# A two-layer decoder trunk on one core: four norm sums as fp32r products, one low part made by VectorE, one Pool split held back

## The chip, the core and the metric

The kernel runs on one core of a Trainium2 chip. TensorE (PE) multiplies, VectorE (DVE) and GpSimd (POOL) work elementwise, ScalarE (ACT) applies functions and copies, SyncE (SP) issues most transfers. The metric is the device time of one execution in microseconds, and of several executions their median.

## What is computed

The reference is a trunk of two layers on a sequence of 1024 positions and a model width of 1024, all in float32:

```python
h = x
for layer in range(2):
    hn = rms_norm(h, norm_mix[layer])
    h = h + (mixer_ab(hn, ...) if layer == 0 else mixer_c(hn, ...))
    h = h + conv_ffn(rms_norm(h, norm_ffn[layer]), ...)
return rms_norm(h, norm_final)
```

`rms_norm(x, g)` is `x * rsqrt(mean(x*x) + 1e-6) * g` over the 1024 features. `mixer_ab` is one input projection, eight heads of dilated attention (A), four heads of gated linear attention in chunks (B), and one output projection. `mixer_c` is a projection with GELU, a causal 128x128 mixing of positions per channel group, a gate and an output projection. `conv_ffn` is an up projection to 2 x 2816, a causal convolution of width 3, a SiLU gate and a down projection.

## The kernel before, in words

**Layout.** Activations stand transposed: features on the 128 partitions, eight tiles `k` of 128 features, 1024 positions in the free dimension. `x` holds the residual stream. A product of float32 accuracy is made of three fp32r products: each operand is split into a high part (rounded to fp32r) and a low part (the difference), and `cross` (L923) adds high x high, high x low and low x high, for two halves of 512 positions each. So every weight tile is split before use: its high part `w_hi` (four slots of 128x1024) by POOL or ScalarE, its low part `w_lo` by POOL with a subtraction (`split`, L626; `low_part`, L635; in the FFN `low`, L692). Activations are split by ScalarE (`high`, L2462) and VectorE (`act_low`, L1646).

**A norm.** The scaling by `rstd` is applied after the product, so that the products with `x * gain` can start before the statistic is there. ScalarE squares the tiles into `sq` and, for the first, `acc` (L2466); VectorE adds them up into `acc` (`accumulate`, L1638). TensorE then sums over the partitions and spreads the sum to all of them by multiplying `ones` (128x128) with `acc`, in f32, one product for each half (`sum_squares`, L953; for the third norm it is written out at L1567 to L1571). VectorE turns the PSUM sum into a variance in `sq` (`norm_var`, L1623; L2330), ScalarE makes a first guess of `rstd` with Ln and Exp (`guess`, L2455), and VectorE refines it in three steps (`norm_refine`, L1628). There are four such norms: `norms[0]` ahead of the first mixer, `norms[1]` ahead of the first FFN, `norms[2]` ahead of mixer C, `norms[3]` ahead of the second FFN. The final norm is done in its own way (`last_sum`, L1523) and is not touched.

**Order.** Each engine's program is written out by hand, and the engines meet by counting semaphores; nothing is planned at run time. What stands around the change:

- Start (`norms[0]`). ScalarE makes the high parts of the eight activation tiles and, after the first of them, the high part of the first weight tile (L2480); POOL makes its low part (L655), which TensorE wants at `weight_low(0)` (L1104). VectorE's first work is the eight `act_low` (L1656), then the additions. POOL's further splits wait until `acc` is done (L657). TensorE does the first k projection by hand (L1101 to L1117), then the q projection, `b_project("q", 0, 0, 6)` (L1118), with the sum of squares behind tile k = 6 of 0 to 7; before the v projection it waits for the variance (L1119), since the sum stands in the PSUM banks that v writes.
- Attention. POOL's splits of the output weights (`N_WO`, L675 to L680) stand behind one another; the third, slot 2, waits for six low parts of activations (`WO.lo`). In the last head pair VectorE forms `a_quad` (`statistics_by_quadrant`, L1934, the first step of the semaphore `A.st` for that pair), and TensorE moves it with eight small products (`move_statistics`, L1270).
- FFN (`norms[1]`, `norms[3]`). `first(0)` and `first(1)` (L1429) are two whole tiles of the up projection; in `first(1)` the sum of squares stands behind k = 1. Then follow 21 pairs of tiles (`pair`, L1455), which are computed with seven products of half tiles each in place of eight: P1, P2, P6, P5, P7, P3, P4 in this order. Each pair has four weight slots with a low part by POOL each: GA (needed by P1), GB (by P6), GC (by P7), GD (by P4). The pair's weights and activations are combined first: POOL makes sums and differences of weight blocks (L715 to L723), VectorE those of activation blocks in `combine` (L2105), once per FFN for four blocks j. ScalarE's program around pair 1 is: high part of GA (L2770), high parts of the combined activations (`t_high(3)`), `guess(norm)`, high part of GB (`high_b(1)`, L2806). VectorE's is: `accumulate` of the last tile, `combine(3)`, `norm_var`, four `low34` (L2127), `norm_refine`. P1 of pair 1 waits for the variance (L1458). The load of pair 2's weights is issued once GC of pair 1 is done (L575).
- Mixer C (`norms[2]`). The sum of squares stands between the third and fourth tile of v (L1567); the additions come in halves of 512 positions. `rstd` is wanted two tiles later (L1574).

## Time and profile before

| what | value |
|---|---|
| median of 3 runs | 2076.26 us (2075.77 to 2076.27) |
| the profiled execution's own time | 2073.93 us |
| its span | 2072.1 us |
| PE busy | 2058.5 us (99%), 10196 products |
| DVE, ACT, POOL busy | 1380.6, 915.3 and 886.7 us |
| mean granted clock of TensorE | 0.998 |

The profile is of one execution. The span runs from its first to its last instruction. In rows of the timeline the columns are the start in us from the start of the span, the duration in us, the engine, the line of the kernel, the operation, the tiles that are written and read, their shapes, the count, and in brackets the idle time of the engine before it with what ended it. PEld is TensorE's load of the stationary operand. An f32 product of 512 columns is recorded as two passes, one of fp32r as a single one. Each product's start is exact; its end is modelled, so the distance of two starts tells what a product costs.

### The profile page before, as it was taken

What the parts mean: (1) busy time and instruction counts of PE and PEld (TensorE: products, weight loads), DVE (VectorE), ACT (ScalarE), POOL (GpSimd) and SP (SyncE); (2) the same over time, 40 slices, a digit from 0 to 9 for tenths busy, and PEclk for the clock granted to TensorE, in tenths of its full rate; (3) what the DMA queues carried; (4) which work ended last, traced back from release to release, by engine and by line L of the source; (5) the groups of instructions that cost most, each with busy time, mean ns of one, the idle gap of its engine ahead of it and who ended that gap; (6) DMA issues with size and microseconds to landing.
All of it is one profiled execution on the core that took longest, in us unless ns stands there. A gap on an engine that the chain in (4) does not pass through costs nothing.

```text
span 2072.1 us, 26319 instructions
## 1 busy us (share of the span) xinstructions
PE 2058.5 (99%) x10196; PEld 1705.5 (82%) x10196; DVE 1380.6 (67%) x1728; ACT 915.3 (44%) x1275; POOL 886.7 (43%) x454
## 2 busy tenths in 40 slices
PE   9999999999999999999999999999999999999997
PEld 7888888888888888888888888888888888888886
DVE  7669866656965556557999404538865556567988
ACT  4231666835544444444435330225544444453444
POOL 4332112233787777850002322444877877730000
PEclk9999999999999999999999999999999999999999
DMA  4111011132222221229982111113321221249872
GB/s 171 41 31 42 21 32 32 32 123 92 103 82 81 92 92 62 92 89 329 389 296 85 57 46 31 51 41 122 112 84 69 92 92 65 88 151 387 300 278 82
DMA packets 95165, 235.95 MB, mean 114 GB/s; under 512 B 10113, under 2 KB 12482, under 8 KB 95042
## 3 DMA queue, kind: packets, MB, share of 16 engines
q1 hardware_dynamic: 93170, 229.54, 31.1%
q10 hardware_dynamic: 1872, 4.74, 0.6%
q8 instruction: 81, 1.33, 0.3%
q14 instruction: 42, 0.34, 0.1%
HBM read 198.59 MB, written 35.65 MB: 113 GB/s over the span
## 4 chain that ended last, share of the span: by engine, by line
PE 96%; DVE 2%; issue 0%; DMA 0%; POOL 0%; ACT 0%; SPq 0%; DVEq 0%
PE ps L1450 13%; PE ps L1452 13%; PE ps L1451 13%; PE ps L1486 7%; PE ps L1487 7%; PE ps L1484 7%; PE ps L929 7%; PE ps L932 6%; PE ps L935 6%; PE ps L1157 2%; PE ps L1159 2%; PE ps L1158 2%; PE ps L1555 1%; PE ps L1556 1%; PE ps L1557 1%; PE ps L1250 1%
## 5 line engine op out<-in xcount | busy, mean ns | idle before, releaser
L631 POOL TENSOR_TENSOR w_hi<-w_raw,ones 128x1024 fp32r<-128x1024 f32 x52 | 102.1, 1963 | 666.6 <-PE ps L935 224.8
L1450 PE MATMUL ps<-t_hi,w_hi 128*128 128x512 f32 x672 | 261.4, 389 | 0.0
L1451 PE MATMUL ps<-t_lo,w_hi 128*128 128x512 f32 x672 | 261.4, 389 | 0.0
L1452 PE MATMUL ps<-t_hi,w_lo 128*128 128x512 f32 x672 | 261.4, 389 | 0.0
L695 POOL TENSOR_TENSOR w_lo<-w_sum,w_hi 128x1024 fp32r<-128x1024 f32 x84 | 248.7, 2964 | 14.1 <-ACT w_hi L2798 14.1
L1484 PE MATMUL ps<-d_hi 128*128 128x512 f32 (+1 forms) x632 | 242.2, 383 | 0.0
L1487 PE MATMUL ps<-d_hi,d_lo 128*128 128x512 f32 (+1 forms) x632 | 241.6, 382 | 0.0
L1486 PE MATMUL ps<-d_lo,d_hi 128*128 128x512 f32 (+1 forms) x632 | 241.6, 382 | 0.0
L695 POOL TENSOR_TENSOR w_lo<-w_raw,w_hi 128x1024 fp32r<-128x1024 f32 x84 | 157.6, 1876 | 160.7 <-ACT w_hi L2798 146.9
L1450 PE MATMUL ps<-act_hi,w_hi 128*128 128x512 f32 x504 | 196.1, 389 | 0.0
L1451 PE MATMUL ps<-act_lo,w_hi 128*128 128x512 f32 x504 | 196.1, 389 | 0.0
L1452 PE MATMUL ps<-act_hi,w_lo 128*128 128x512 f32 x504 | 196.1, 389 | 0.0
L929 PE MATMUL ps<-act_hi,w_hi 128*128 128x512 f32 x592 | 184.9, 394 | 0.0
L932 PE MATMUL ps<-act_lo,w_hi 128*128 128x512 f32 x592 | 182.4, 389 | 0.0
L935 PE MATMUL ps<-act_hi,w_lo 128*128 128x512 f32 x592 | 182.3, 389 | 0.0
L2795 ACT ACTIVATE snap<-ps 128x512 f32<-128x512 f32 x126 | 75.3, 598 | 226.0 <-PE ps L1452 225.8
L637 POOL TENSOR_TENSOR w_lo<-w_raw,w_hi 128x1024 fp32r<-128x1024 f32 x56 | 145.3, 2594 | 63.8 <-ACT w_hi L2645 32.6
L2798 ACT ACTIVATE w_hi<-w_sum 128x1024 fp32r<-128x1024 f32 x84 | 89.2, 1062 | 152.8 <-PE ps L1452 122.0
L1452 PEld LDWEIGHTS ps<-t_hi,w_lo 128*128 128x128 f32 x672 | 126.1, 188 | 26.2
L1451 PEld LDWEIGHTS ps<-t_lo,w_hi 128*128 128x128 f32 x672 | 126.1, 188 | 26.2
L1450 PEld LDWEIGHTS ps<-t_hi,w_hi 128*128 128x128 f32 x672 | 126.1, 188 | 26.1
L2163 DVE SCALAR_TENSOR_TENSOR ps<-fz,cw,ps 128x1023 f32<-128x1023 f32 x88 | 113.3, 1287 | 48.0 <-ACT ps L2782 48.0
(350 smaller groups left out, 4404.5 us busy)
## 6 DMA issues: line engine op xcount, KB each, us to landing
w_raw<-w_up SPq DMA_DIRECT2D x44, 1024.0 KB, 4.9
d_ring<-w_dn SPq DMA_DIRECT2D x146, 256.0 KB, 7.6
d_ring<-g_kept SPq DMA_DIRECT2D x124, 256.0 KB, 9.5
g_kept<-gst SPq DMA_DIRECT2D x44, 512.0 KB, 3.6
w_raw<-w_in SPq DMA_DIRECT2D x24, 512.0 KB, 3.6
chain_a<-g_kept SPq DMA_DIRECT2D x44, 256.0 KB, 8.5
x_kept<-x SPq DMA_DIRECT2D x16, 512.0 KB, 8.3
x<-x_kept SPq DMA_DIRECT2D x16, 512.0 KB, 10.5
```

The source lines that it names most:

```text
L637: pool.tensor_tensor(w_lo[:, slot, :], w_raw[:, parity, :], w_hi[:, slot, :].bitcast(F32), ALU.subtract).then_inc(s_wsplit, 1)
L695: pool.tensor_tensor(w_lo[:, slot, cols].rearrange("p (a j c) -> p a j c", j=4, c=P), src, w_hi[:, slot, cols].bitcast(F32).rearrange("p ( ...
L929: pe.matmul(out[:, cols], wh, act_hi_k[:, cols], start=first, stop=False)
L932: pe.matmul(out[:, cols], wh, act_lo_k[:, cols], start=False, stop=False)
L935: ins = pe.matmul(out[:, cols], wl, act_hi_k[:, cols], start=False, stop=last)
L1450: pe.matmul(out, wh, bh, start=(fresh and j == 0), stop=False, skip_group_check=True)
L1451: pe.matmul(out, wh, bl, start=False, stop=False, skip_group_check=True)
L1452: ins = pe.matmul(out, wl, bh, start=False, stop=(j == 3), skip_group_check=True)
L1484: pe.matmul(out, w[:, 0, wcols], w[:, 1, cols], start=(s == 0 and i not in (D6, D7)), stop=False, skip_group_check=True)
L1486: pe.matmul(out, w[:, 0, wcols], g[:, 1, cols], start=False, stop=False, skip_group_check=True)
L1487: return pe.matmul(out, g[:, 0, wcols], w[:, 1, cols], start=False, stop=(s == NBLK - 1), skip_group_check=True)
L2163: dve.scalar_tensor_tensor(fc[:, 1:S], fz[:, t, 0:S - 1], cw[:, layer, tile, 1:2], fc[:, 1:S], ALU.mult, ALU.add).then_inc(F.tap.sem, 1)
```

## The change

`acc` is split like every other operand. A new buffer `acc_parts` (two tiles of 128x1024, in the place of `sq`) holds its high part, a copy by ScalarE (`sum_high`), and its low part, a subtraction by VectorE (`sum_low`). The sum over the partitions becomes two fp32r products for each half, `ones_r` with the high and with the low part. `ones` is the same memory, read as float32. In the FFNs the sum moves from behind k = 1 to behind k = 3 of `first(1)`, and in the first norm from behind k = 6 to behind k = 7. `sum_low` stands inside `combine(3)` of VectorE, and `sum_high` ahead of `t_high(3)` of ScalarE. The low part of the first weight tile is made by VectorE between its first and second `act_low`; POOL only waits for it. POOL's third output split waits for `a_quad` of the last head pair (`A.st` at 8 x 4 - 7 = 25) as well. The semaphores of Ln and Exp are merged into one of two counts.

```diff
+        acc_parts = sb("acc_parts", 172, [P, 2, S], F32R)
-        ones = sb("ones", 202.5, [P, P])
+        ones_r = sb("ones_r", 202.5, [P, P], F32R)
+        ones = ones_r[:].bitcast(F32)
...
@@ POOL
-            low_part(0, 0, 2)
+            pool.wait_ge(s_wsplit, N_B + 1)
             plain(1, 1)
             pool.wait_ge(*past(norms[0].acc, KT - 1))
...
-            plain(N_WO + 2, 2, (WO.lo, 6))
+            plain(N_WO + 2, 2, (WO.lo, 6), (A.st, 8 * NHP - 7))
...
@@ TensorE
             def sum_squares(norm, out):
-                pe.wait_ge(*past(norm.acc, KT - 1))
+                pe.wait_ge(*past(norm.parts, 2))
                 for h in range(2):
-                    ins = pe.matmul(out[:, h * HALF:(h + 1) * HALF], ones[:], acc[:, h * HALF:(h + 1) * HALF],
-                                    start=True, stop=True)
+                    cols = slice(h * HALF, (h + 1) * HALF)
+                    pe.matmul(out[:, cols], ones_r[:], acc_parts[:, 0, cols], start=True, stop=False)
+                    ins = pe.matmul(out[:, cols], ones_r[:], acc_parts[:, 1, cols], start=False, stop=True)
                 ins.then_inc(norm.sum.sem, 1)
...
-            b_project("q", 0, 0, 6)
+            b_project("q", 0, 0, 7)
...
-                        if t == 1 and k == 1:
+                        if t == 1 and k == 3:
                             sum_squares(norm, slot2(0))
...
+            pe.wait_ge(*past(norms[2].parts, 2))
             for h in range(2):
-                pe.wait_ge(*past(f0.hacc[h], KT - 1))
-            for h in range(2):
-                ins = pe.matmul(ps[:, 3 + 4 * h, :], ones[:], acc[:, LAST[h]], start=True, stop=True)
+                pe.matmul(ps[:, 3 + 4 * h, :], ones_r[:], acc_parts[:, 0, LAST[h]], start=True, stop=False)
+                ins = pe.matmul(ps[:, 3 + 4 * h, :], ones_r[:], acc_parts[:, 1, LAST[h]], start=False, stop=True)
...
@@ VectorE
+            def sum_low(norm):
+                dve.wait_ge(*past(norm.parts, 1))
+                dve.tensor_tensor(acc_parts[:, 1, :], acc[:], acc_parts[:, 0, :].bitcast(F32), ALU.subtract
+                                  ).then_inc(norm.parts.sem, 1)
...
-            for k in range(KT):
+            act_low(norms[0], 0)
+            dve.wait_ge(s_wdma[0], 16)
+            dve.wait_ge(s_whi, 2)
+            dve.tensor_tensor(w_lo[:, 0, :], w_raw[:, 0, :], w_hi[:, 0, :].bitcast(F32), ALU.subtract).then_inc(s_wsplit, 1)
+            for k in range(1, KT):
                 act_low(norms[0], k)
             for k in range(KT):
                 accumulate(norms[0], k)
+            sum_low(norms[0])
             norm_var(norms[0], slot2(2))
...
-                def combine(j):
+                def combine(j, between=None):
...
                     dve.tensor_tensor(t34_raw[j][:, 0, :], b22, b12, ALU.subtract).then_inc(F.tadd.sem, 1)
+                    if between is not None:
+                        sum_low(between)
...
-                combine(3)
+                combine(3, norm)
...
+            sum_low(norms[2])
             dve.wait_ge(*past(norms[2].sum, 1))
...
@@ ScalarE
+            def sum_high(norm):
+                act.activation(acc_parts[:, 0, :], acc[:], ACT.Copy).then_inc(norm.parts.sem, 1)
...
+            act.wait_ge(*past(norms[0].acc, KT - 1))
+            sum_high(norms[0])
             guess(norms[0])
...
+                act.wait_ge(*past(norm.acc, KT - 1))
+                sum_high(norm)
                 t_high(3)
...
+            for h in range(2):
+                act.wait_ge(*past(f0.hacc[h], KT - 1))
+            sum_high(norms[2])
             guess(norms[2])
```

## Rows read from the trace of the kernel before

**Rows 1.** The page's chain that ended last, shares of the span by engine.

```profile
PE 96%; DVE 2%; issue 0%; DMA 0%; POOL 0%; ACT 0%; SPq 0%; DVEq 0%
```

**Rows 2.** TensorE's waits: in total, times, longest, in us.

```profile
PE ps L1270 <- DVE a_quad L1934: 0.6, 1, 0.6
PE ps L1080 <- POOL w_lo L637: 0.4, 1, 0.4
```

**Rows 3.** Timeline of VectorE and TensorE around the third norm's sum.

```profile
1157.76 0.68 DVE L2324 TENSOR_TENSOR acc<-acc,sq 128x512 f32<-128x512 f32 x1
...
1161.10 0.39 PE L1557 MATMUL ps<-w_hi,act_lo 128*128 128x512 f32 x1
1161.33 1.88 PE L1570 MATMUL ps<-acc,ones 128*128 128x512 f32 x4
...
1163.28 0.40 PE L1556 MATMUL ps<-w_lo,act_hi 128*128 128x512 f32 x1
```

**Rows 4.** Timeline of POOL and VectorE from 7 to 20 us.

```profile
7.61 2.39 POOL L637 TENSOR_TENSOR w_lo<-w_raw,w_hi 128x1024 fp32r<-128x1024 f32 x1 [4.08 <-ACT w_hi L2480]
8.91 2.17 DVE L1648 SCALAR_TENSOR_TENSOR act_lo<-x,gain,act_hi 128x1024 fp32r<-128x1024 f32 x1 [1.24 <-ACT act_hi L2463]
...
16.73 2.09 POOL L631 TENSOR_TENSOR w_hi<-w_raw,ones 128x1024 fp32r<-128x1024 f32 x1 [6.72 <-DMA w_raw<-w_in]
16.99 2.91 DVE L1648 SCALAR_TENSOR_TENSOR act_lo<-x,gain,act_hi 128x1024 fp32r<-128x1024 f32 x1
...
18.89 3.24 POOL L637 TENSOR_TENSOR w_lo<-w_raw,w_hi 128x1024 fp32r<-128x1024 f32 x1
```

**Rows 5.** Timeline of VectorE, POOL and TensorE around the first norm's sum.

```profile
29.97 1.23 DVE L1644 TENSOR_TENSOR acc<-acc,sq 128x1024 f32<-128x1024 f32 x1
...
31.54 1.89 POOL L631 TENSOR_TENSOR w_hi<-w_raw,ones 128x1024 fp32r<-128x1024 f32 x1 [9.41 <-DVE acc L1644]
...
33.45 1.88 PE L956 MATMUL ps<-acc,ones 128*128 128x512 f32 x4
...
35.37 1.22 DVE L1626 TENSOR_SCALAR sq<-ps 128x1024 f32<-128x1024 f32 x1 [4.17 <-PE ps L956]
...
36.65 0.30 PEld L929 LDWEIGHTS ps<-act_hi,w_hi 128*128 128x128 f32 x2 [0.35 <-DVE sq L1626]
```

**Rows 6.** POOL's third output split (timeline), and all of line L1934 (`a_quad`).

```profile
424.90 1.90 POOL L631 TENSOR_TENSOR w_hi<-w_raw,ones 128x1024 fp32r<-128x1024 f32 x1 [20.49 <-DVE act_lo L2000]
...
L1934 DVE TENSOR_TENSOR a_quad<-a_class,lmul x4: 280/538/1822, 273.5 to 425.1; 128x128 f32<-128x128 f32 x4
```

**Rows 7.** Timeline around the second norm, then POOL's row of the fourth.

```profile
524.75 2.86 DVE L2115 TENSOR_TENSOR t_raw<-xg_low,t_raw 128x512 f32<-128x512 f32 x1
527.02 1.75 POOL L715 TENSOR_TENSOR w_sum<-w_raw 128x512 f32<-128x512 f32 x1
...
531.48 1.21 DVE L1626 TENSOR_SCALAR sq<-ps 128x1024 f32<-128x1024 f32 x1
...
536.06 1.05 ACT L2798 ACTIVATE w_hi<-w_sum 128x1024 fp32r<-128x1024 f32 x1
...
537.12 1.21 DVE L2127 TENSOR_TENSOR t_lo<-t_raw,t_hi 128x1024 fp32r<-128x1024 f32 x1
537.19 3.41 POOL L695 TENSOR_TENSOR w_lo<-w_sum,w_hi 128x1024 fp32r<-128x1024 f32 x1 [2.21 <-ACT w_hi L2798]
...
540.95 0.19 PEld L1450 LDWEIGHTS ps<-t_hi,w_hi 128*128 128x128 f32 x1
...
1449.25 3.38 POOL L695 TENSOR_TENSOR w_lo<-w_sum,w_hi 128x1024 fp32r<-128x1024 f32 x1 [2.23 <-ACT w_hi L2798]
```

**Rows 8.** The page's row of the loads of `w_up`, and the start of pair 2.

```profile
w_raw<-w_up SPq DMA_DIRECT2D x44, 1024.0 KB, 4.9
...
551.94 2.40 POOL L695 TENSOR_TENSOR w_lo<-w_raw,w_hi 128x1024 fp32r<-128x1024 f32 x1 [0.25 <-ACT w_hi L2798]
...
554.55 0.19 PEld L1450 LDWEIGHTS ps<-act_hi,w_hi 128*128 128x128 f32 x1
```

More of the change, by code:

```diff
@@ L238, in past @@
             return count.sem, count.first + n
-        PER_NORM = {"sq": KT, "acc": KT - 1, "hi": KT, "lo": KT, "sum": 1, "var": 3, "ln": 1, "exp": 1, "rstd": 1}
+        PER_NORM = {"sq": KT, "acc": KT - 1, "hi": KT, "lo": KT, "sum": 1, "var": 3, "guess": 2, "rstd": 1,
+                    "parts": 2}
         Norm = namedtuple("Norm", ("col", *PER_NORM))
@@ L1630, in norm_refine @@
                 v, t = sq[:, 0, :], sq[:, 1, :]
-                dve.wait_ge(*past(norm.exp, 1))
+                dve.wait_ge(*past(norm.guess, 2))
                 dve.scalar_tensor_tensor(t, v, -0.5, rstd[:], ALU.mult, ALU.mult).then_inc(norm.var.sem, 1)
@@ L2457, in guess @@
                 act.wait_ge(*past(norm.var, 1))
-                act.activation(rstd[:], sq[:, 0, :], ACT.Ln).then_inc(norm.ln.sem, 1)
-                act.wait_ge(*past(norm.ln, 1))
-                act.activation(rstd[:], rstd[:], ACT.Exp, scale=-0.5).then_inc(norm.exp.sem, 1)
+                act.activation(rstd[:], sq[:, 0, :], ACT.Ln).then_inc(norm.guess.sem, 1)
+                act.wait_ge(*past(norm.guess, 1))
+                act.activation(rstd[:], rstd[:], ACT.Exp, scale=-0.5).then_inc(norm.guess.sem, 1)
+            def sum_high(norm):
+                act.activation(acc_parts[:, 0, :], acc[:], ACT.Copy).then_inc(norm.parts.sem, 1)
             def high(norm, k):
```

## Prediction

> **What bounds the kernel now.** I read the chain of work that ended last first: TensorE holds 96% of it [rows 1]. Then TensorE's waits: whole-kernel stalls are small, and the two that this change can touch are 0.6 us for VectorE's `a_quad` and 0.4 us for the first low part [rows 2]. Everywhere else TensorE issues back to back, so time comes off in two ways only: fewer slots on TensorE, or one of these stalls; and it is lost when some operand becomes late. So for each edit I ask when TensorE arrives and when its operand is ready.
>
> **The price of a product.** Around the third norm's sum [rows 3] one fp32r product of 512 columns takes a slot of 0.227 us (1161.10 to 1161.33). The f32 sum starts at 1161.33 and the second product behind it at 1163.28: 1.95 less one slot is 1.72 us for its two f32 products (four records, two passes each). The new sum is four fp32r products: 4 x 0.227 = 0.91 us. Each norm gives back 0.82 us of TensorE if nothing waits. For that ScalarE makes a rounded copy of `acc` (one pass of 128x1024, 1.05 us as its copy of a weight slot [rows 7]) and VectorE a subtraction with both inputs in SBUF (1.23 us as the last `acc` addition [rows 5]).
>
> **What VectorE and POOL do to each other.** This decides the sum, and the rows show it [rows 4]. POOL's split runs 16.73 to 18.82. VectorE's `act_lo`, asked for at 16.99, ends at 19.90, 1.08 us after POOL is done. POOL's next, asked for at 18.89, ends at 22.13, 2.23 us after VectorE. So an operation of VectorE with two SBUF inputs and one of POOL take turns as wholes, and what was begun first keeps the turn. One with a PSUM input does not: the variance at 35.37 takes 1.22 us [rows 5] beside a POOL subtraction.
>
> The Trainium skill, "SBUF — State Buffer", section "Who interferes with whom", says so as a rule: whichever starts first holds the shared port pair for the whole instruction and the other fully blocks; the trace agrees with its 2.91 us in place of the 1.21 us of an unhindered two-input step [rows 7]. It speaks against a change that puts two-input subtractions onto VectorE beside POOL's splits. Were the port shared by halves instead, the second norm below would lose under 1 us and the total would be near 2076.
>
> **First norm, and the first low part.** POOL's low part ends at 10.00 (7.61 + 2.39); VectorE can make it from 7.6 (POOL began at 7.61, when the high part was there) to 8.8, and its next `act_lo` starts at 8.91 anyway [rows 4], so it costs VectorE nothing and TensorE starts about 0.6 us sooner (0.4 us of wait [rows 2] and the restart). This carries to the end of the q projection. There the sum moves from behind k = 6 to behind k = 7, and the v projection still waits for the variance, whose PSUM banks it overwrites. Before, the sum starts at 33.45, the variance at 35.37, and v at 36.65 after a wait of 0.35 [rows 5]. After: q ends near 34.0. `acc` is done at 31.20 (29.97 + 1.23), or 0.4 sooner if the last `act_lo`, freed by the earlier low part, begins just ahead of POOL's 16.73 and not at 16.99 [rows 4]; the copy ends near 31.9 to 32.3. POOL's split (31.54 to 33.43) is then in its turn, so the subtraction ends at 34.1 to 34.5. The four products and the variance follow, v starts at 36.7 to 37.2. So the 0.6 and the 0.82 are both swallowed by the wait for the variance: +0.05 us, range -0.1 to +0.5.
>
> **The Pool split that waits.** POOL's `w_hi` at 424.90 begins 0.2 us before `a_quad` (425.1), which takes 1.82 us where its shortest of four took 0.28 [rows 6]. It is what TensorE waits 0.6 us for [rows 2]. With the added wait POOL stands until `a_quad` is done near 425.4, so the split ends some 0.6 us later. Behind it in POOL's queue stands only the next output split, which waits long for the combined heads. The split is used only when output tile 2 starts, near 447. Gain 0.6 us; it costs at worst an `act_lo` of VectorE 0.5 us, which has 1 us and more of cover. -0.6 us.
>
> **Second and fourth norm.** Here lies the doubt. The sum itself is fine: the copy is done near 525.4, POOL's low part holds the turn until 527.07, the subtraction ends near 528.15, and TensorE, which now asks two k later (2 x 6 slots), arrives at 528.3. But what stands behind the new subtraction on VectorE? Before, three two-input steps of `combine(3)` alternate with POOL's sums: `t_raw` asked for at 524.75 ends at 527.61, when POOL's 527.02 sum goes on [rows 7]. The new subtraction takes the first turn (1.08 us), POOL's sum the next (1.16). So everything behind is 2.23 us later, the variance too: 531.48 becomes 533.7. From the end of the variance hang Ln, a table load, Exp, and then ScalarE's high part of the second slot of pair 1; POOL's low part of that slot starts 4.50 us after the variance's end (532.69 to 537.19) [rows 7]. At 537.12, 0.07 us ahead of it, VectorE has begun a two-input `t_lo`, and POOL ends at 540.60. After the change the `t_lo` come one place earlier, but `rstd`'s first refinement stands in that place (four times 1.13 us behind), and wins by the same 0.05 us. So POOL's low part is at 540.60 + 2.27 = 542.87. TensorE loads weights for that product at 540.95 [rows 7], 0.3 us of cover; now it would arrive 0.82 us sooner and wait 2.8 us. Net: not -0.82 but about +1.9 us (542.92 for 540.95, less 0.1 of overlap at the restart). The fourth norm has the same rows 912.06 us later (POOL's low part 3.38 us from 1449.25): again +1.9 us.
>
> Is it lost for good? TensorE has no idle time behind it to give back. Next in line is pair 2's first low part, 551.94 to 554.34 against a weight load at 554.55 [rows 8], 0.2 us of cover. It hangs on a load that is issued when POOL has done pair 1's third low part, which is some 2.25 us late, so it comes near 556.4; TensorE, 1.85 late, arrives at 556.40. Even: 0 to +0.1.
>
> **Third norm.** POOL is idle. `acc` ends at 1158.44 [rows 3], copy to 1159.5, subtraction to 1160.8, TensorE loads the sum's weights at 1161.10: 0.3 us of cover. `rstd` is sooner by as much. -0.82 us.
>
> **The sum.** +0.05 - 0.6 + 1.9 - 0.82 + 1.9 = +2.4 us. The profiled execution took 2073.93 us for a span of 2072.1, so its span becomes 2074.5; the median of the runs is 2076.26, 2.3 us above that execution, and I add the difference there: **2078.7 us**. Alone, this case spans 2077.5 to 2080.
>
> **Rivals.** (A) The subtractions do not delay the splits: POOL wins the turns, or ScalarE's high part comes in time. Then all of the second to fourth norm count: -0.6 - 3 x 0.82 = -3.1, 2073.2 us. For it: the sum's own moves leave no wait on TensorE. Against: 0.3 us of cover only, in both norms.
> (B) POOL's request comes just ahead of the refinement. It is 0.05 us that decides. Then the low part is ready at 541.7, the stall is 1.6 us, each norm nets +0.85 and the sum is +0.3: 2076.6 us. Against: before, VectorE won this place in both norms.
> (C) Slower: pair 2's weights. Their load (1 MB, median 4.9 us to landing [rows 8]) is issued 2.25 us late with cover gone; every us that it takes above the 5.1 it now does is paid on both layers. From 0.9 us more it is over +4.2: 2080.6 us and more.
> (D) The change does not do what it says: fp32r products against `ones` cost what the f32 did. Then the third norm's 0.82 stays, the second and fourth are still set by the low part: +3.2, 2079.5 us.
>
> **Chances.** Forecast 0.50, A 0.20, B 0.15, C 0.10, D 0.05. The range of 8 in 10 leaves out C and the tail of A: 2073.0 to 2080.3. About 0.2% (4.15 us) is what a measurement can tell from no change. No case but C lies beyond it, and A if the first norm's 1.4 us came through too: faster 0.04, same 0.85, slower 0.11.
>
> **What the profile after would show.** If right: the variances of the second and fourth norm start some 2.2 us later against the first product of `first(1)`; POOL's low part L695 of pair 1 is 3.4 us long and ends 2.3 us later; TensorE's waits list a new line, TensorE for POOL's `w_lo` L695, twice 2.5 to 2.8 us; the wait for `a_quad` is gone; the wait for the variance before v is near 1.5 us; the third sum takes 0.91 us and nothing waits. Four f32 records per norm are replaced by four fp32r ones. What makes it wrong: turns that are granted in another order than asked for, or a wait of the low part that I placed behind the variance and that is free.

## The result and the profile after

| what | before | after |
|---|---|---|
| median of 15 runs each | 2075.51 us (2073.80 to 2078.10) | 2079.19 us (2077.31 to 2081.04) |
| profiled execution, own time and span | 2073.93, 2072.1 us | 2077.84, 2076.0 us |
| mean granted clock of TensorE | 0.998 | 0.997 |

The ratio after to before is 1.0016, with a 95% interval of 1.0008 to 1.0023: about 3.3 us slower. The interval (1.7 to 4.8 us) leaves out no change, but it does not say whether the change is over or under 0.2% (4.15 us). The profiled execution is 3.9 us longer than that of before, which is a quick one: only one of the fifteen runs of before is below 2073.93 us.

Both programs issue the same products of the projections and pairs, so I set each product's start in the trace after against the start of the same product before and read off the shift (minus is sooner). All shifts below are made that way. In the table a row is the change of the shift over that stretch, and the last row is the shift at the end.

| stretch | predicted, us | after, us | second execution of after, us |
|---|---|---|---|
| start, up to the attention's last pair | +0.05 | -0.24 | -0.16 |
| wait for `a_quad` | -0.6 | -0.83 | -0.84 |
| second norm, behind P6 of pair 1 | +1.9 | +1.85 | +1.89 |
| third norm | -0.82 | -0.86 | -0.86 |
| fourth norm, behind P6 of pair 1 | +1.9 | +1.82 | +1.80 |
| sum of these | +2.4 | +1.7 | +1.8 |
| a stretch at half clock at 1176 us | not foreseen | +1.6 | +1.6 |
| late transfers (pair 2 of the second FFN, down projections) | 0 to +0.1 | +0.6 | +0.9 |
| end | +2.4 | +3.9 | +4.4 |

(The row of late transfers sums rounded shifts at several places.)

TensorE's waits in the kernel after (us in total, times, longest). The waits for `a_quad` and for the first low part [rows 2] are gone. A stall at P6 of pair 1, which comes twice, and the wait of 1.3 us for the variance before v are new (the wait for `tiny`, 1.1 us at the very start, is in both kernels). The releaser of P6 is not inferred ("issue"); the next rows show it.

```profile
PE ps L1454 <- issue: 4.3, 2, 2.1
PE ps L932 <- DVE sq L1630: 1.3, 1, 1.3
PE ps L1089 <- DVE tiny L1661: 1.1, 1, 1.1
```

Timeline of the kernel after around the second norm (start, us, engine, line, operation, tiles, shapes, count, idle time before), VectorE, then POOL, then TensorE; it answers to [rows 7]:

```profile
524.31 2.80 DVE L1652 TENSOR_TENSOR acc_parts<-acc,acc_parts 128x1024 fp32r<-128x1024 f32 x1 [0.54 <-ACT acc_parts L2480]
527.03 1.77 DVE L2131 TENSOR_TENSOR t_raw<-xg_low,t_raw 128x512 f32<-128x512 f32 x1
...
532.66 1.21 DVE L1630 TENSOR_SCALAR sq<-ps 128x1024 f32<-128x1024 f32 x1
...
538.34 1.21 DVE L1636 SCALAR_TENSOR_TENSOR sq<-sq,rstd 128x1024 f32<-128x1024 f32 x1
```

```profile
523.47 2.56 POOL L698 TENSOR_TENSOR w_lo<-w_raw,w_hi 128x1024 fp32r<-128x1024 f32 x1 [6.84 <-ACT w_hi L2792]
525.99 2.26 POOL L718 TENSOR_TENSOR w_sum<-w_raw 128x512 f32<-128x512 f32 x1
...
538.37 6.72 POOL L698 TENSOR_TENSOR w_lo<-w_sum,w_hi 128x1024 fp32r<-128x1024 f32 x2 [4.47 <-ACT w_hi L2822]
```

```profile
539.32 0.39 PE L1456 MATMUL ps<-act_hi,w_lo 128*128 128x512 f32 x1
541.85 0.47 PE L1454 MATMUL ps<-t_hi,w_hi 128*128 128x512 f32 x1 [2.14 <-issue]
```

The new subtraction asks at 524.31, waits for POOL's low part (done 526.03) and ends at 527.11; POOL's sum, asked for at 525.99, ends at 528.25. Everything of VectorE behind them is late: the variance starts at 532.66 against 531.48 before, while TensorE at that place was 1.08 us sooner than before, so 2.26 us late by its own clock. The refinement (538.34) is 0.03 us ahead of POOL's low part (538.37), which therefore takes 3.4 us (two equal ones in the row) and is done near 541.75. TensorE starts P6 at 541.85; without a stall it would have started at 539.55.

The late variance holds TensorE once more before that. P1 of pair 1 waits for it: its weight load starts 0.12 us behind the variance's end (533.87), and the shift moves by 0.3 us there, in both FFNs. This adds nothing to the loss, because P6 starts when POOL's low part is done in any case.

```profile
533.99 0.19 PEld L1454 LDWEIGHTS ps<-act_hi,w_hi 128*128 128x128 f32 x1 [0.46 <-issue]
```

The start of the kernel after: VectorE's first low part, then the two engines' turns behind `acc`, then the sum on TensorE and the wait before v [rows 4, 5]:

```profile
7.41 1.23 DVE L1667 TENSOR_TENSOR w_lo<-w_raw,w_hi 128x1024 fp32r<-128x1024 f32 x1
...
31.60 2.19 DVE L1652 TENSOR_TENSOR acc_parts<-acc,acc_parts 128x1024 fp32r<-128x1024 f32 x1 [1.13 <-ACT acc_parts L2480]
35.15 1.22 DVE L1630 TENSOR_SCALAR sq<-ps 128x1024 f32<-128x1024 f32 x1 [1.35 <-PE ps L961]
```

```profile
33.94 0.47 PE L960 MATMUL ps<-acc_parts,ones_r 128*128 128x512 f32 x1
...
36.43 0.73 PE L932 MATMUL ps<-act_hi,w_hi 128*128 128x512 f32 x2 [1.31 <-DVE sq L1630]
```

Half-way through the q projection TensorE was 0.9 us sooner than before, and the shorter sum saves 0.8 us more; v starts at 36.43 against 36.65, so all but 0.2 us of both went into the wait for the variance.

### The profile page after: what moved, and what is told of

The parts are those of the page before. It is cut to its first block, busy times and chain, and to the rows that moved or that the text cites. A ratio compares the mean times of both kernels' runs of the same rounds, so it can differ in the third digit from the quotient of the medians.

```text
span 2076.0 us, 26329 instructions
## 1 busy us (share of the span) xinstructions
PE 2057.3 (99%) x10196; PEld 1705.6 (82%) x10196; DVE 1382.9 (67%) x1733; ACT 918.9 (44%) x1279; POOL 885.9 (43%) x453
## 4 chain that ended last, share of the span: by engine, by line
PE 94%; DVE 3%; DMA 2%; issue 1%; SPq 1%; ACT 0%; DVEq 0%
PE ps L1454 13%; PE ps L1455 13%; PE ps L1456 13%; PE ps L932 7%; PE ps L935 6%; PE ps L938 6%; PE ps L1488 6%; PE ps L1491 6%; PE ps L1490 6%; PE ps L1161 2%; PE ps L1163 2%; PE ps L1162 2%; PE ps L1561 1%; PE ps L1560 1%; PE ps L1559 1%; DMA d_ring<-g_kept 1%
## 5 line engine op out<-in xcount | busy, mean ns | idle before, releaser
L634 POOL TENSOR_TENSOR w_hi<-w_raw,ones_r 128x1024 fp32r<-128x1024 f32 x52 | 102.8, 1977 | 671.2 <-PE ps L938 224.3
```

## Experiments

The experiments take the kernel after or before and change one thing. Shifts are those of the profiled execution against the profiled execution of before. Where an experiment has a median, it is set against runs of before of its own series.

### The FFN sums as before

```diff
-                        if t == 1 and k == 3:
-                            sum_squares(norm, slot2(0))
+                        if t == 1 and k == 1:
+                            sum_squares_f32(norm, slot2(0))
...
-                combine(3, norm)
+                combine(3)
...
-                act.wait_ge(*past(norm.acc, KT - 1))
-                sum_high(norm)
```

> The changed kernel with the sums of the second and fourth norm as before: f32 products of acc behind k = 1, no copy and no subtraction in the FFNs. Theory of turns (VectorE's subtraction and POOL's splits alternate, the variance and all behind it come 2.2 us late, TensorE stands 2.5 us before the P6 product of pair 1): both stalls go, TensorE passes each FFN's start without gain or loss, so against the changed kernel -1.8 us at each, 3.7 us in all; the span is some 1.5 to 2 us below the kernel before. Rival, the clock: if the changed kernel is slower mainly because TensorE's clock falls for some 3 us behind the third norm, that stretch stays, and the kernel is no faster than before by more than 0.5 us.

Median 2073.50 us (10 runs) against 2074.77 for before (25 runs); ratio 0.9994, 0.9985 to 1.0004. Both stalls at P6 are gone (shift -0.79 before and behind P6 of the first, -1.58 of the second). The wait for `a_quad` gave -0.84 and the third norm -0.86, as in the kernel after. So the stalls and their cost belong to what the change does in the two FFN norms. The end is -1.15 where I expected -1.5 to -2: 0.4 us is lost at the last down projection. There is no stretch at half clock in this trace. The median alone is not clear of no change.

### Only the high part of the FFN sums

This kernel leaves the low part of the sum out of both FFN norms (the sum is less exact); copy, place (k = 3) and the wait are kept.

```diff
-                combine(3, norm)
+                combine(3)
...
-                            sum_squares(norm, slot2(0))
+                            sum_squares_high(norm, slot2(0))
```

> The changed kernel, but in the second and fourth norm the sum is taken of acc's high part alone: ScalarE's copy and the place behind k = 3 stay, VectorE's subtraction and the products with the low part are left out. Theory of turns: the subtraction alone makes the variance late, so VectorE's steps stand as in the kernel before, POOL's low part of pair 1's second slot ends at its old time, and TensorE, which now comes 1.3 us earlier (two products in place of 1.72 us of f32), waits for it only about 1 us in place of 2.5; shift of TensorE at that product against the kernel before about 0 in each FFN in place of +1.8. Rival, the copy or the later place of the sum makes the variance late: the stall stays at 2.5 us or more, since TensorE comes still earlier.

Own time 2072.66 us. The sum itself gives 1.32 us (two products in place of the f32 ones), and TensorE then stands 0.7 us at P6, since it arrives that much ahead of a low part that is not late: the shift goes from -0.67 to -0.90 behind the start of pair 2 in the first FFN, from -1.75 to -1.32 in the second, where pair 2's weights also arrived 1 us later than in the profile of before. ScalarE's copy and the later place of the sum cost nothing that would explain a stall of 2.5 us; what is gone with it is VectorE's subtraction.

### The subtraction alone

From the kernel of "the third sum alone" below (no copy, the FFN sum f32 behind k = 1), with one useless subtraction in `combine(3)`:

```diff
                     dve.tensor_tensor(t34_raw[j][:, 0, :], b22, b12, ALU.subtract).then_inc(F.tadd.sem, 1)
+                    if between is not None:
+                        dve.wait_ge(*past(between.acc, KT - 1))
+                        dve.tensor_tensor(acc_parts[:, 1, :], acc[:], acc[:], ALU.subtract)
```

> The same kernel (only the third sum made of parts, the FFN sums f32 behind k = 1), with one subtraction of two SBUF inputs (acc less acc, 128x1024, its result unused) put into VectorE's combine(3), where the kernel after has its low part of acc. No copy of ScalarE, no later place of the sum, no other product. My theory: the subtraction and the POOL turn that it lets in are by themselves what makes the variance and everything behind it 2.2 us late, so the low part of pair 1's second slot is done near 541.7 less what the earlier start gives, and TensorE, which is 1.74 us sooner than before there, stands 1.5 to 2.5 us at P6: the shift behind P6 goes from -1.74 to between -0.2 and +0.7, again in the second FFN. Rival: the stall came from the sum's later place and ScalarE's copy ahead of t_high; then there is no stall at P6 and the shifts are -1.74 and -2.6 as without the subtraction.

One instruction of VectorE, whose result nobody reads, brings the stall back: the shift goes from -1.75 to +0.11 at P6 of the first FFN and from -0.75 to +1.09 of the second, +1.86 and +1.84. VectorE and POOL of this kernel:

```profile
522.98 3.40 DVE L2137 TENSOR_TENSOR acc_parts<-acc 128x1024 fp32r<-128x1024 f32 x1
526.30 1.78 DVE L2139 TENSOR_TENSOR t_raw<-xg_low,t_raw 128x512 f32<-128x512 f32 x1
...
531.95 1.21 DVE L1638 TENSOR_SCALAR sq<-ps 128x1024 f32<-128x1024 f32 x1
```

```profile
537.66 6.74 POOL L699 TENSOR_TENSOR w_lo<-w_sum,w_hi 128x1024 fp32r<-128x1024 f32 x2 [4.47 <-ACT w_hi L2826]
```

and of the same kernel without it (its second series):

```profile
529.71 1.21 DVE L1638 TENSOR_SCALAR sq<-ps 128x1024 f32<-128x1024 f32 x1
```

```profile
535.41 6.74 POOL L699 TENSOR_TENSOR w_lo<-w_sum,w_hi 128x1024 fp32r<-128x1024 f32 x2 [2.22 <-ACT w_hi L2825]
```

The variance moves by 2.24 us and the low part by 2.25 us: one turn of the subtraction and one of POOL, as the step of the prediction had it (2.23 us), and not the 1.2 us that the instruction takes by itself. POOL's low part takes about 3.4 us with the subtraction and without it.

### The tie between the refinement and POOL

```diff
                 for j in range(4):
                     low34(j)
+                dve.memset(tiny[:, 63:64], 0.0)
                 norm_refine(norm)
```

> The changed kernel with one memset of a single column on VectorE ahead of the first refinement of rstd in each FFN. In the changed kernel that refinement begins 0.03 us before POOL asks for its low part of pair 1's second slot. Theory of turns, what asks first holds the turn: the memset takes some 0.06 us or more, POOL is first, its low part takes 2.4 us and not 3.4, and each stall falls from 2.5 to about 1.4 us: some 2.2 us less in all than the changed kernel. Rival, VectorE gets the next turn anyway, or the memset is hidden in the end of the step before: nothing changes, within 0.3 us in the trace at this product.

Median 2079.65 us, ratio 1.0021 (1.0012 to 1.0031). The memset did not do what I wanted. It takes 0.06 us and the trace shows it inside the refinement's time, with the refinement still starting at 538.33, so each stall stays at 2.1 us:

```profile
538.33 1.22 DVE L1636 SCALAR_TENSOR_TENSOR sq<-sq,rstd 128x1024 f32<-128x1024 f32 x1
538.35 0.06 DVE L2166 MEMSET tiny<- 128x1 f32 x1
```

```profile
538.35 3.39 POOL L698 TENSOR_TENSOR w_lo<-w_sum,w_hi 128x1024 fp32r<-128x1024 f32 x1 [4.48 <-ACT w_hi L2823]
```

So it said nothing on what happens when POOL is first; VectorE was 0.02 us ahead and had the turn. The next one does it by a wait:

```diff
+                dve.wait_ge(*past(F.wlo, lows(1, GB)))
                 norm_refine(norm)
```

> The kernel after, but VectorE's refinement of the second and fourth norm's rstd waits until POOL has made the low part of pair 1's second slot (it is the operation that took the turn ahead of POOL by 0.03 us). My theory of turns: POOL's subtraction then takes 2.3 us in place of 3.38, is done near 540.65, and the stall of TensorE at P6 is 1.1 us shorter in both FFNs: each FFN nets +0.7 in place of +1.84, the end is +1.6 against before in place of +3.9 (2 us less again if no three-microsecond stretch at half clock falls into this execution). The refinement ends 3.4 us later, at 543; nothing of TensorE should hang on it, since P1 of pair 1 needs the bank and not rstd. Rival one: the low part's length has nothing to do with VectorE's turn; then it stays at 3.4 us and the stall as it is. Rival two: the stall shrinks, and rstd's being late holds up the evictions of the first tiles, so that P7 or P3 waits instead: the net stays near +1.8.

```profile
541.15 3.40 DVE L1636 SCALAR_TENSOR_TENSOR sq<-sq,rstd 128x1024 f32<-128x1024 f32 x1 [2.36 <-POOL w_lo L698]
```

```profile
538.74 4.72 POOL L698 TENSOR_TENSOR w_lo<-w_sum,w_hi 128x1024 fp32r<-128x1024 f32 x2 [4.48 <-ACT w_hi L2823]
```

```profile
541.22 0.47 PE L1454 MATMUL ps<-t_hi,w_hi 128*128 128x512 f32 x1 [1.10 <-issue]
```

POOL's low parts take 2.36 us each in place of 3.36, TensorE's wait falls from 2.14 to 1.10 us. The shift over the second norm is -0.68 to +0.13, over the fourth -0.31 to +0.46: +0.8 in place of +1.8 each. That is the +0.85 that rival B gave for the lost tie. A further +0.4 to +0.5 comes at the start of pair 2 of each FFN. The end is +0.9 and there is no stretch at half clock in it; own time 2074.83 us. The stall is thus two parts: a turn of the subtraction with the POOL turn behind it, and the turn that VectorE takes ahead of POOL's low part. Only the first is new. The kernel before pays the second as well, for a `t_lo` in place of the refinement: its low part takes 3.41 us too [rows 7]. The added wait wins back 1.0 us that the kernel before also loses, and it does not remove what the change costs.

The Trainium skill, "SBUF — State Buffer", section "Who interferes with whom", calls the port pair that VectorE and GpSimd share an exclusive lock, says that a VectorE instruction with two SBUF inputs contends with a GpSimd one that reads SBUF, and that issue order decides who blocks. The trace agrees: the same POOL subtraction takes 2.36 us with VectorE held back and 3.4 us with VectorE 0.02 to 0.03 us ahead.

### ScalarE's high part ahead of the guess

```diff
-                guess(norm)
                 high_b(1)
+                guess(norm)
```

> The changed kernel with ScalarE making the high part of pair 1's second weight slot ahead of the first guess of rstd, not behind it. It waits for the end of the second whole tile, about 534, and so is ready near 535.3 in place of 538.3. Theory of turns plus chain (the low part hangs on the variance only through ScalarE's order): POOL's low part is ready near 538.5, before TensorE asks at 539.3, the stall of 2.5 us goes in both FFNs, and the kernel is 4 to 4.8 us faster than the changed kernel, unless the later rstd (about 2 us) makes the first evictions late. Rival, the stall only moves: the products P7 or P4 of pair 1 wait for their low parts or for rstd, and less than 2 us is won.

Median 2077.30 us, ratio 1.0014 (1.0005 to 1.0024): still slower than before. The low part starts at 535.48 and P6 now waits 0.7 us, for ScalarE's copy of a PSUM bank. But the third slot's high part now comes behind the guess: POOL, idle for 3.45 us until it is there, starts that slot's low part only at 542.16, and pair 2 starts late:

```profile
555.62 0.50 PE L1454 MATMUL ps<-act_hi,w_hi 128*128 128x512 f32 x1 [1.04 <-POOL w_lo L698]
```

A second stall of 1.0 us, 1.9 us in the second FFN (where the load of pair 2's weights also came 1 us later), takes most of what the first gave: net +1.8 and +2.7 us. The 4 to 4.8 us that I expected did not come; the rival, a stall that moves, did. This order of ScalarE makes another low part late; whether some other order would make none late was not tried.

### Two edits by themselves

The kernel before with the added wait of the Pool split only:

```diff
-            plain(N_WO + 2, 2, (WO.lo, 6))
+            plain(N_WO + 2, 2, (WO.lo, 6), (A.st, 8 * NHP - 7))
```

> The kernel before, with nothing changed but the added wait of POOL's third output split for a_quad. My theory: the wait of TensorE for a_quad (0.6 us) goes and its restart with it: products behind 437 us are 0.8 us sooner and stay so to the end, span 2071.3 or, with the late transfer of the down projection, 2071.7. Rival: in the kernel after it was the other arrival times that moved POOL out of the way; alone, the split still meets a_quad or meets the next step of VectorE: no shift, or less than 0.3 us.

The shift goes from -0.11 to -0.94 at this place. `a_quad` takes 0.29 us in place of 1.82 [rows 6] and POOL starts behind it:

```profile
424.97 0.29 DVE L1934 TENSOR_TENSOR a_quad<-a_class,lmul 128x128 f32<-128x128 f32 x1
```

```profile
425.43 1.89 POOL L631 TENSOR_TENSOR w_hi<-w_raw,ones 128x1024 fp32r<-128x1024 f32 x1 [21.21 <-DVE a_quad L1934]
```

The gain comes whole in each of the eleven traces with this edit (0.84 us from just before this place to just behind it), and in neither of the other two, which have 0.04 and 0.01. This execution's end is nevertheless +1.13: +1.62 of it is a stretch at half clock at 1176 us, although nothing of the kernel is changed there, and +0.3 a late transfer.

The kernel before with the first low part by VectorE only:

```diff
-            low_part(0, 0, 2)
+            pool.wait_ge(s_wsplit, N_B + 1)
```

(and the subtraction of the change in VectorE).

> The kernel before, with nothing changed but the first weights' low part made by VectorE. My theory: products of the first projection are sooner by about 0.6 to 0.8 us, the f32 sum behind k = 6 with them, so v starts 0.6 to 0.8 us sooner and the end too: the 0.35 us wait for the variance stays as it is. Rival: acc is late enough to hold the sum, and v starts where it did.

The shift is -0.34 from v on, where I expected -0.6 to -0.8. But TensorE waited 0.6 us for an `act_hi`, and the kernel before, in a second execution, has -0.42 there by an earlier load alone. One execution does not settle this edit.

### The third sum alone is made of parts

The first norm as before too: f32 behind k = 6, no copy, no subtraction. Kept are VectorE's first low part, the Pool split that waits, and the third norm's sum.

```diff
-            b_project("q", 0, 0, 7)
+            b_project("q", 0, 0, 6)
...
-            sum_low(norms[0])
...
-            act.wait_ge(*past(norms[0].acc, KT - 1))
-            sum_high(norms[0])
```

> The kernel after, but the first norm's sum and both FFN norms' sums are f32 products of acc as before (behind k = 6 and behind k = 1), with no copy and no subtraction there. Kept are VectorE's low part of the first weights, the Pool split that waits, and the fp32r sum of the third norm. My theory: in the kernel after, TensorE's gain at the start (0.8 us half-way through the q projection) was swallowed by the wait for the variance, because copy and subtraction lengthened the way from acc to the sum. With the sum as before nothing lengthens it, so the gain is carried on: v starts 0.8 us sooner than before. With 0.84 for the wait for a_quad and 0.86 for the third sum that is -2.5 us against before; the 0.45 us that the down projection of the second layer lost behind the undisturbed kernels may be lost again. Median ratio 0.9988 to 0.9990, and 0.6 us below the kernel with only the FFN sums undone. Rival: the gain of the start is swallowed in any case, by acc or by the load of the next weights: ratio 0.9994 as with the FFN sums alone undone.

> The same kernel as the one in which only the third norm's sum is made of parts and the other three are f32 as before, with VectorE's first low part and the held-back Pool split kept, timed again in more rounds. In its trace all products were 2.6 us sooner than in the profiled execution of before, yet the median of its runs was only 1.4 us lower. My theory: the gain of 2.6 us is the same in every execution (0.8 start, 0.84 statistic, 0.86 third sum), and what blurs it is a stretch of three microseconds at half clock (1.6 us each) that some executions have behind the small products or a stall; the before's profiled execution had none. Ratio 0.9988 (2.5 us), between 0.9984 and 0.9994. Rival: the kernel's real gain is 1.4 us or less because something in it brings such stretches or late transfers more often: ratio 0.9994 or above.

First series: 2073.30 us (11 runs) against 2074.71 (15), ratio 0.9993 (0.9984 to 1.0002). Second: 2072.67 us (11 runs) against 2075.53 (15), ratio 0.9987 (0.9978 to 0.9996). The first misses the 0.9988 to 0.9990 that I expected, and its interval holds 1; the second alone is clear of no change. The mean of the two is 2.1 us. In both traces the shifts are alike: v starts 0.83 and 0.91 us sooner and nothing waits before it, then -0.84 and -0.86 follow and the end is -2.64 and -2.67 (spans 2069.5 and 2069.4 us). The wait for the variance before v is gone, and its line too; the second series:

```profile
32.55 1.88 PE L960 MATMUL ps<-acc,ones_r 128*128 128x512 f32 x4
33.86 1.03 PE L933 MATMUL ps<-act_hi,w_hi 128*128 128x512 f32 x2
...
35.74 0.73 PE L933 MATMUL ps<-act_hi,w_hi 128*128 128x512 f32 x2
```

That shows where the start's gain had gone in the kernel after: into the longer way from `acc` to the variance. The start bears this out over all traces. Just ahead of `a_quad`, the seven that have the first norm's sum in parts stand at -0.26 to +0.16, with a median of +0.05; the three that have VectorE's first low part and the f32 sum (the two here and the one with the subtraction alone) stand at -0.90 to -0.95. So in the first norm, too, the parts and their later place are worse than the f32 sum, by about 0.9 us. This version has what is good in the change. Against before its medians are 1.4 and 2.9 us lower, its traces 2.6 and 2.7 us. Of that I call the 0.84 and 0.86 us shown, and the first low part's share (0.4 to 0.9 us, depending on the load) only bounded.

### Both kernels once more

> The kernel after, unchanged, one more profiled execution. My theory: the two stalls at P6 (2.5 us each) and the wait for the variance of 1.3 us belong to the kernel and come again within 0.1 us; the stretch at half clock behind the one-column products at 1174 to 1176 us does not, it falls there or behind a stall, once, twice or not at all. Without any the end is +2.3 against before, and 1.6 more for each. Rival: the stretch at 1176 belongs to the change and is there again.

The stalls came again: 2.11 us at P6 of both FFNs, 1.3 before v. So did the stretch at half clock at 1176 us, which was the rival's sign and not mine. The fourth norm's pair 2 was late by 0.72 us: POOL waited 3.72 us for the load of its weights, where it waited 2.75 us in the profile of before and 2.88 us in the first one of after.

```profile
1465.86 1.29 POOL L718 TENSOR_TENSOR w_sum<-w_raw 128x512 f32<-128x512 f32 x1 [3.72 <-DMA w_raw<-w_up]
```

That is the loss that rival C named, but the late load is not the change's: in the kernel before, executed again, the same wait is 3.93 us, and in the one with the first low part alone 4.21 us (0.5 and 0.8 us lost).

```profile
1462.36 1.30 POOL L715 TENSOR_TENSOR w_sum<-w_raw 128x512 f32<-128x512 f32 x1 [3.93 <-DMA w_raw<-w_up]
```

> The kernel before, unchanged, one more profiled execution. My theory: the waits for a_quad (0.6 us) and at the start come again; the runs of before lie between 2073.8 and 2078.1 us, and the profiled one was among the lowest because it had no stretch at half clock. This one shows, if its time is over 2075, one such stretch of 1.6 us at one of the places seen in the other traces, or the late transfer of the down projection near 1904 us. Rival: the spread of before has nothing to do with the clock, and an execution above 2075 shows full clock everywhere.

Own time 2074.88 us, 0.95 more than the first execution of before, with no stretch at half clock that the other lacks. Its shifts are -0.43 at the start (a load), +0.66 near 990 to 1160, +0.5 at pair 2 of the second FFN and +0.3 at the last down projection. Its waits, each 0.2 to 0.4 us, are for low parts whose loads came late:

```profile
PE ps L1484 <- DVE d_lo L2259: 0.4, 1, 0.4
PE ps L1450 <- POOL w_lo L695: 0.2, 1, 0.2
```

A single execution of this kernel thus moves by about 1 us at the end, and by 0.4 us at its start, without a change.

## Why the prediction came out as it did

**Right, and shown.** The direction, 2078.7 against 2079.19 us, and the mechanism of the second and fourth norm. Its steps hold one by one: the subtraction first, then POOL, hence all behind 2.23 us later (2.26 in the kernel after, 2.24 with the subtraction alone); 4.50 us from the variance's end to POOL's low part (4.50: 533.87 to 538.37); the refinement wins the tie by 0.03 us where the forecast said 0.05; the low part takes 3.4 us. The stall itself was forecast as 2.8 us and is 2.3 us (541.85 less 539.55; the list of waits says 2.1), for the most part because the forecast had no wait for the variance at P1, where TensorE had lost 0.3 us already. Behind the stall this makes no difference. With TensorE's 0.8 us subtracted this gives +1.85 and +1.82 for a forecast of +1.9. The rivals fall: A needed the splits not delayed, B needed POOL to win, which only the kernel with the added wait shows (+0.8 per norm for +0.85). C needed pair 2 to pay for its load being issued later, and in the profile of after TensorE loses nothing at pair 2 in either FFN. D falls by the third norm, where the four products take 0.91 us:

```profile
1162.20 0.39 PE L1573 MATMUL ps<-acc_parts,ones_r 128*128 128x512 f32 x1
...
1163.11 0.39 PE L1559 MATMUL ps<-w_hi,act_hi 128*128 128x512 f32 x1
```

**Right in size, wrong in detail.** The Pool split: 0.83 us and not 0.6. I took the wait of the list [rows 2] and left out what I had added at the start, the restart behind a wait. The first norm: q ended at 33.91 (34.0 forecast) and the subtraction at 33.79 (34.1 to 34.5), v started at 36.43, a little before the 36.7 to 37.2 forecast. The two executions of after, -0.24 and -0.16, lie just outside my range (-0.1 to +0.5), but the seven traces with this start have their median at the +0.05 that I named, and the start moves by 0.4 us on its own. The wait before v is 1.3, near the 1.5 named. Two sums are slips without weight: pair 2's first low part comes out at 556.6 by my own numbers (554.34 + 2.25) and not 556.4, and rival C's time at 2080.5 and not 2080.6.

**Not foreseen.** The sum of my terms was +2.4; the terms themselves came to +1.7 and +1.8. The median nevertheless moved by 3.7 us and the ratio says 3.3 (1.7 to 4.8). The rest is in the traces: 1.6 us at half clock, and 0.6 to 0.9 us of late transfers. I had a price for the transfers (rival C) and none for the clock. The transfers are not shown to be the change's: the kernel before, executed again, is 1.4 us later at three such places than in its first execution, which all shifts are counted from. So the closeness of 2078.7 to 2079.19 is in part luck: my shift was 1.3 us too small, and the median of before from which I counted (2076.26, three runs) is 0.75 us above that of the fifteen.

**Open, but with a lean.** Whether the change makes the half-clock stretch more frequent. In the traces it was in both executions of after, in the one with a memset (twice, behind the stalls), and not in the two of before; but the kernel with the Pool wait alone had it at 1176 us with nothing changed there, and those with the tie undone or ScalarE's order changed had none, though they have the same third norm. The runs without a trace say more, since each has its mean granted clock. A trace with one such stretch reads 0.997 or 0.998, with two 0.996, with none 0.998 or 0.999. Of the 15 runs of the kernel after, 9 read 0.997 or less, and of the 10 with the memset, 9; of 55 runs of before in the three later series 6 do, of the 10 with ScalarE's order changed 2, of the 10 with the FFN sums as before 2, and of the 22 with the third sum alone 2. The mean is 0.9971 for after and 0.9981 for before. My estimate from these: 0.0009 of 2076 us is 1.9 us of clock, or 3.8 us more at half clock for each run, somewhat over one stretch of 3.4 us, at a price of 1.8 us. With +1.7 to +1.8 us of terms that makes 3.5 to 3.6 us, for a measured 3.3 by the ratio and 3.7 by the medians. The estimate is rough: the readings are rounded to 0.001, the last 6 to 9 us of every trace are at the lower level too, and the runs of before are from other series than those of after. Why the stretch comes in one execution and not in the next, and which stall or place brings it, no run shows.

## What to carry to other kernels

Price an instruction on VectorE by the turns that it brings, not by its duration: 1.2 us of two-input subtraction ahead of a statistic put 2.25 us onto everything behind it, because it let POOL's next operation in as well. Before shortening a sum on a TensorE that never idles, count the work on other engines that it buys the shorter sum with, and ask which operand has the least cover behind it; here 0.86 us saved on TensorE cost 2.7 us in each of two norms, was swallowed in the first, and was kept only in the third, where POOL is idle. And where an edit bundles several, the ledger of shifts by product tells which to keep.

## What the runs showed of the hardware

**The clock.** The granted clock of TensorE is at the upper of its two levels (2.4 GHz) from 8 us to TensorE's last products, but in some executions it falls to the lower (1.2 GHz) for 3.4 us, behind very small products or behind a stall: once in each of the two traces of after and in the one with the Pool wait alone, twice in the one with the memset, not at all in the ten others. In the kernel after it fell behind sixteen one-column products (1174.08, 1.94 us); seven products then took slots of 0.427 us in place of 0.227. The kernel before has the same sixteen products, and there it did not fall. Windows of the kernel after, then of before, with the same work (window, its length, busy time and count of PE, PEld, DVE, ACT, POOL, granted clock, DMA share, GB/s):

```profile
1174.00:1176.00 2.00, 2.00 (x18) 1.91 (x17) 0.00 (x0) 0.00 (x0) 0.00 (x0) 1.00 0.00 0
1176.00:1178.00 2.00, 2.00 (x7) 1.57 (x7) 1.30 (x2) 1.71 (x4) 0.00 (x0) 0.59 0.00 0
1178.00:1180.00 2.00, 2.00 (x7) 1.57 (x6) 0.00 (x0) 1.94 (x5) 0.00 (x0) 0.56 0.00 0
```

```profile
1174.00:1176.00 2.00, 2.00 (x18) 1.92 (x17) 0.00 (x0) 0.00 (x0) 0.00 (x0) 1.00 0.00 0
1176.00:1178.00 2.00, 2.00 (x10) 1.66 (x10) 1.30 (x2) 1.72 (x4) 0.00 (x0) 1.00 0.00 0
```

In the kernel with the memset it fell behind both stalls of 2.1 us at P6 instead (the windows behind the stall of the first FFN and of the second), at about 1.6 us each, on top of the stall's own price:

```profile
542.00:545.50 3.50, 3.50 (x10) 2.75 (x10) 3.47 (x2) 0.00 (x0) 3.50 (x2) 0.58 0.00 0
...
1457.00:1460.50 3.50, 3.50 (x10) 2.74 (x10) 3.46 (x2) 0.00 (x0) 3.50 (x2) 0.55 0.02 5
```

```profile
134.00:137.00 3.00, 3.00 (x13) 1.70 (x12) 2.51 (x3) 1.36 (x2) 2.92 (x2) 1.00 0.00 0
```

**A moved stall.** With ScalarE's order changed, 1.5 us less at P6 came with a stall of 1.0 us at the next pair, 15 us later, and of 1.9 us in the second FFN, where a late load has a part in it.
